# Feed-forward layers: the low parts of the first tile pairs' weights move from VectorE to GpSimd

## What is computed

```python
h = modulate(rms_norm(x, g_ffn1[l]), sh1, sc1)
x = x + 0.5 * ga1[:, None, :] * swiglu(h, w_gate1[l], w_up1[l], w_down1[l])
# swiglu(h, w_gate, w_up, w_down) = (silu(h @ w_gate) * (h @ w_up)) @ w_down
```

## Time and profile before

| | us |
|---|---|
| median of three runs | 2234.31 |
| the profiled execution | 2234.3 |
| its span, first to last instruction | 2232.6 |
| TensorE busy in the span | 2202.2 |
| VectorE busy | 1559.5 |
| ScalarE busy | 1071.6 |
| GpSimd busy | 903.2 |

### The profile page before, as it was taken

The page is one execution under the profiler, slowest core; times in us unless marked ns, Lnnn a source line. Parts: engine busy times, 40 slices in busy tenths (PEclk is TensorE's granted clock), DMA queues, the critical chain, the costliest instruction groups (busy, mean ns, idle before and its releaser), DMA issues.

```text
span 2232.6 us, 29463 instructions
## 1 busy us (share of the span) xinstructions
PE 2202.2 (99%) x10472; PEld 1814.6 (81%) x10472; DVE 1559.5 (70%) x2116; ACT 1071.6 (48%) x2028; POOL 903.2 (40%) x782
## 2 busy tenths in 40 slices
PE   7999999999999999999999999999999999999998
PEld 6888888888887888888787887888778888888887
DVE  7976767578878757732899998578785454547765
ACT  5533333333454553344899898425443333333344
POOL 0044555400122655544557656447205555530013
PEclk9999999999999999999999999999999999999999
DMA  7156565374561533444814065323223222347454
GB/s 281 73 194 221 210 216 202 137 295 165 188 224 50 162 125 137 152 166 141 226 53 119 15 161 152 120 95 142 104 87 126 89 106 103 109 162 262 148 177 160
DMA packets 152033, 338.01 MB, mean 151 GB/s; under 512 B 14224, under 2 KB 36880, under 8 KB 151888
## 3 DMA queue, kind: packets, MB, share of 16 engines
q1 hardware_dynamic: 150624, 333.57, 44.3%
q10 hardware_dynamic: 1264, 2.56, 0.5%
HBM read 247.28 MB, written 86.64 MB: 150 GB/s over the span
## 4 chain that ended last, share of the span: by engine, by line
PE 82%; DVE 11%; ACT 3%; issue 2%; DMA 1%; POOL 1%; SPq 0%; DVEq 0%; ACTq 0%; POOLq 0%
PE ps L3184 11%; PE ps L3185 11%; PE ps L3186 11%; PE ps L3332 6%; PE ps L3330 6%; PE ps L3331 6%; PE ps L3411 4%; PE ps L3413 4%; PE ps L3412 4%; PE ps L3538 3%; PE ps L3563 2%; PE ps L3564 2%; PE ps L3523 2%; PE ps L3142 2%; PE ps L3144 2%
## 5 line engine op out<-in xcount | busy, mean ns | idle before, releaser
L3184 PE MATMUL ps<-r_main,r_z 128*128 128x512 f32 x1232 | 482.0, 391 | 6.1 <-DVE r_main L2212 3.4
L1964 POOL TENSOR_TENSOR r_z<-f_main,r_z 128x512 fp32r<-128x512 f32 x213 | 304.6, 1432 | 446.6 <-ACT r_z L1231 446.6
L3185 PE MATMUL ps<-r_main,r_z 128*128 128x512 f32 x1232 | 480.3, 390 | 0.0
L3186 PE MATMUL ps<-r_main,r_z 128*128 128x512 f32 x1232 | 480.3, 390 | 0.0
L1231 ACT CAST r_z<-f_main 128x512 fp32r<-128x512 f32 x254 | 155.8, 621 | 346.7 <-PE ps L3186 277.5
L3184 PEld LDWEIGHTS ps<-r_main,r_z 128*128 128x128 f32 x1232 | 231.9, 188 | 60.2 <-DVE r_main L2212 4.4
L3186 PEld LDWEIGHTS ps<-r_main,r_z 128*128 128x128 f32 x1232 | 231.8, 188 | 48.2
L3185 PEld LDWEIGHTS ps<-r_main,r_z 128*128 128x128 f32 x1232 | 231.8, 188 | 47.6 <-issue 0.2
L3330 PE MATMUL ps<-r_main 128*128 128x512 f32 x604 | 235.8, 390 | 0.0
L3332 PE MATMUL ps<-r_main 128*128 128x512 f32 x604 | 235.0, 389 | 0.0
L3331 PE MATMUL ps<-r_main 128*128 128x512 f32 x604 | 235.0, 389 | 0.0
(11 more groups left out here) (385 smaller groups left out, 4497.7 us busy)
## 6 DMA issues: line engine op xcount, KB each, us to landing
act_d<-f_main SPq DMA_DIRECT2D x154, 256.0 KB, 2.0
f_main<-act_d SPq DMA_DIRECT2D x70, 512.0 KB, 4.9
f_main<-in_ada SPq DMA_DIRECT2D x56, 512.0 KB, 5.2
f_main<-in_wg SPq DMA_DIRECT2D x20, 1024.0 KB, 5.0
f_main<-in_wu SPq DMA_DIRECT2D x20, 1024.0 KB, 5.0
f_w<-in_wo SPq DMA_DIRECT2D x40, 512.0 KB, 4.0
f_main<-in_wmix SPq DMA_DIRECT2D x18, 1024.0 KB, 5.4
f_e<-in_we SPq DMA_DIRECT2D x10, 1024.0 KB, 5.6
```

The lines of the kernel that those rows point to most:

```text
L1964: pool.tensor_tensor(prod_lo_t[slot], source_of(g), prod_hi_t[slot].bitcast(F32), ALU.subtract).then_inc(s["wl"], 1)
L3184: pe.matmul(out, wh, hi, start=start, stop=False, skip_group_check=True)
L3185: pe.matmul(out, wh, lo, start=False, stop=False, skip_group_check=True)
L3186: return pe.matmul(out, wl, hi, start=False, stop=stop, skip_group_check=True)
```

## The change

VectorE's `first_pair`, used by both layers, loses its 20 `weight_low` calls (`g` = 8 to 27). GpSimd's program starts its loop at 8 in the first layer, and at 0 without a break in the second. The values computed are the same. VectorE still makes `g` = 0 to 7 of the first layer. In `first_pair` one `taken` (UP, product 2) also comes before a `weight_sum`.

```diff
-            pool.wait_ge(fsem[0]["wl"], fbase[0]["wl"] + SECOND + 6)
-            for g in range(SECOND + 6, N_PROD):
+            pool.wait_ge(fsem[0]["wl"], fbase[0]["wl"] + PRELUDE)
+            for g in range(PRELUDE, N_PROD):
                 weight_low(0, g)
...
-            for g in range(PRELUDE):
-                weight_low(1, g)
-            pool.wait_ge(fsem[1]["wl"], fbase[1]["wl"] + SECOND + 6)
-            for g in range(SECOND + 6, N_PROD):
+            for g in range(N_PROD):
                 weight_low(1, g)
...
                     if m >= 12:
                         t1_t3(k, m - 12)
-                        if k == 0:
-                            weight_low(f, m - 4)
...
-                for g in range(8, 12) if k == 2 else ():
-                    weight_low(f, g)
                 for i in range(4):
                     x_low(k, 7, i)
-                weight_low(f, 12)
                 weight_sum(f, 1, UP, 3)
...
                 weight_sum(f, 1, UP, 1)
-                weight_low(f, 13)
-                weight_low(f, 14)
                 for i in range(4):
                     x_low(k, 6, i)
                 weight_sum(f, 1, UP, 2)
-                weight_low(f, 15)
-                weight_low(f, 16)
                 x_low(k, 5, 0)
...
-                weight_low(f, 17)
                 taken(f, AT[1, UP, 6])
                 weight_sum(f, 1, GATE, 4)
-                weight_low(f, 18)
                 weight_sum(f, 1, UP, 4)
-                weight_low(f, 19)
                 taken(f, AT[1, GATE, 5])
-                weight_low(f, 20)
-                weight_low(f, 21)
                 taken(f, AT[1, UP, 5])
...
                     act_sum(f, 0, i)
-                weight_low(f, 22)
+                taken(f, AT[1, UP, 2])
                 weight_sum(f, 2, GATE, 2)
-                weight_low(f, 23)
-                taken(f, AT[1, UP, 2])
                 last_quarter(f, 1)
-                for g in (24, 25, 26):
-                    weight_low(f, g)
                 taken(f, AT[1, UP, 4])
                 weight_sum(f, 2, GATE, 4)
-                weight_low(f, 27)
                 taken(f, AT[1, UP, 3])
```

## The result

The changed kernel takes **2244.0 us**, against 2234.31 before: a ratio of 1.0044, 95% interval 1.0028 to 1.006, that is 6.3 to 13.4 us. The prediction said 2244.3. Four of its runs lie between 2243.63 and 2244.22; a fifth took 4104.97 us at a lower granted clock (0.82) and is left out. The profiled execution took 2244.0 as well. Lines of the code have moved: `piece` is now at L3162 to L3164, `t1_t3` at L2221 and L2222, `t2` at L2229, `t4` at L2235, `x_low` at L2209 and L2212, `weight_sum` 3, 1, 2 and 4 at L2245, L2247, L2251 and L2255, `act_sum` at L2269, `taken` at L2295, L2297 and L2303, `plain_taken` at L2360. GpSimd's `weight_low` is still L1964.

A forecast was written before the change was run, and what follows sets the result against it. TensorE was taken as the bound, its few gaps set by VectorE's full list. Adding +5.2 (first layer), +4.1 (second) and +0.8 (restarts), 10.1 us, to 2234.3 gave 2244.3 us, range 2236 to 2249.5.

The forecast's parts named there:

- What bounds: TensorE, busy 99% of the span, waits in eight gaps for VectorE's full list; at most 4.6 us to gain.
- what an added call does to VectorE: A GpSimd subtraction holds up VectorE steps with two SBUF operands, 1.08 us each; steps reading PSUM keep their length.
- The price of 1.08: Microseconds that one VectorE step with two SBUF operands loses when it meets a GpSimd call.
- The first layer's walk: Engine lists followed forward through the first layer's first pair: TensorE lags 1.3, 1.6, 3.9, 4.9 us, in sum +5.2 us.
- restarts: Each TensorE gap costs 0.08 us more before the next start; some ten gaps more, +0.8 us in all.
- The loads: Pair 2's gate weights load later, moving the cast of 22 from 108.00 to 111.8 us; this costs nothing.
- The second layer: First pair of the second layer: low parts 8 to 11 meet an idle VectorE; loss of +4.1 us.
- The 2.0 us that ScalarE's silu steps were to bring: Second layer, products 22 and 23: silu steps behind the late `act_sum` bring 2.0 us, while gaps of 1.1 fall away.
- The number of collisions: VectorE steps held up by GpSimd calls: 14 counted in the first layer, 10 in the second.
- The full hold: Rival, 12%: each VectorE step held up loses GpSimd's whole 1.25 us; 13.5 us in sum, 2247.8 us.
- Half the collisions: Rival, 10%: only plain subtractions held up, or calls mostly meet PSUM steps and idle time; 2237.5 us.
- VectorE relieved: Rival, 9%: the 12.2 us a layer freed on VectorE's list make up for hold-ups; 2230.9 us.

The follow-up runs named there:

- experiments of 1 and 2: 1: kernel before plus useless GpSimd work, reading SBUF 2261.57 us, only writing 2234.27 us; 2: changed kernel, GpSimd writing zeros for low parts 8 to 27, 2230.32 us.
- experiment 2: The changed kernel, but GpSimd's low parts 8 to 27 are two memsets each in place of the subtraction; 2230.32 us, ratio 0.9983.
- the reading version: The kernel before, VectorE making all low parts, plus a useless GpSimd subtraction reading SBUF for each high part 8 to 27; 2261.57 us, ratio 1.0126.

## Why the prediction was right

**What bounds, and what an added call does to VectorE: right, and shown.** The steps beside GpSimd's calls mostly last 1.67 to 1.78 us in place of 0.69 to 0.74, both plain subtractions and scalar_tensor_tensors; steps with an operand in PSUM keep their length, as the 0.69 at 104.62 beside GpSimd's calls of 102.83 to 108.82. The price of 1.08 was 1.04 to 1.1 in the rows at 71.04 and 72.74. The experiments of 1 and 2 take the cause and the move apart: reads without the move cost 28 us, some 8 of them by the clock; the move without reads gains 3.5.

**The first layer's walk, step by step.** `weight_sum` (UP 2) was to start at 92.6 (2.6 after 90.03) and started at 92.92. Product 15 was to start at 95.5 and started at 95.72; the piece in product 20 at 114.5, it came at 114.62; product 24 at 126.8, it came at 127.22; `weight_sum` (GATE 4) at 124.8, and its row reads 124.09 with 1.76 us, so its undisturbed part (0.69) began at 125.2. The predicted lags of 1.6 and 3.9 and the sum of 5.2 are +1.86 at product 18, +4.05 at 21 and +5.57 at 28 in the table above, restarts included. The layer's sum was 5.2 and half of the 0.8 for restarts, 5.6; measured 5.57, or 5.77 where the execution had no lead. The loads were hidden: the cast of 22, which waits for pair 2's weights, was expected at 111.8 and came at 112.05, and its product did not wait.

**The second layer.** Expected 4.1 and 0.4, measured +4.28. Lows 8 to 11 meet no work of VectorE's, as the 5.05 us at 1618.24 show, and product 24's gap is the one at 1681.24. The 2.0 us that ScalarE's silu steps were to bring at products 22 and 23 are the waits of 0.60 and 1.26 at 1672.95 and 1677.17.

**What was luck, and which terms were off.** That 2244.3 met 2244.0 to 0.3 us is luck in part: the interval of the loss is 6.3 to 13.4 us. The sum was 10.1 us; the time shows 9.7, the two layers' losses in TensorE's starts make 10.1, and no run can tell these apart. The restarts, 0.8 of the sum, were measured by no run alone. The stretched steps cost 14.1 and 10.0 us of VectorE's list where 15.1 and 10.8 were counted, because some met only a part of a call (0.92 us at 112.97, 0.48 at 126.38). The number of collisions was right in sum, not in each place: in the first layer the 128x4 step at 68.07 was one of the 14, and low 12's call stretched no step. The walk let GpSimd have its turn after the step that VectorE was in, and low 12 waited for two (2.30 us). That call ended 0.6 us later than one that waits once, VectorE's `x_low` kept their pace, and `weight_sum` (UP 3) paid with its wait of 1.25 at 83.17.

**The rivals.** The full hold (2247.8) falls by the rows: the longest addition to a VectorE step is 1.12 us, most are 1.04 to 1.1. Its total lies only just above the interval (2240.6 to 2247.7). Where the two engines alternate, VectorE's steps start 1.70 us apart (71.04, 72.74, 74.44), while its 0.61 and GpSimd's whole 1.25 one after the other would be 1.86. The Trainium skill, SBUF — State Buffer, section "Who interferes with whom", has the two engines share a port pair under an exclusive lock, the loser fully blocked. The runs agree with it about which operations meet, and that a GpSimd instruction which only writes doesn't disturb a VectorE one with two SBUF inputs (2234.27 against 2233.84), but the measured price is 1.09 of GpSimd's 1.25 to 1.29. Half the collisions falls: 14 and 10 were there, as counted. VectorE relieved falls because the collisions are there; experiment 2 is that rival made real, 2230.32 where it gave 2230.9.

## What to carry to other kernels

Before moving an elementwise step from VectorE to GpSimd, look in the trace for any pair of rows where the two already overlap, and compare a step's duration there with its duration elsewhere; here a moved call saves 0.61 us of VectorE's list and costs 1.08 in it. By the rows a moved call costs VectorE nothing where VectorE waits, reads PSUM, or GpSimd only writes. Where the list of the busiest helper sets the gaps, look at the order in it too: one call put behind another gained 1.1 us a layer in TensorE's starts (too little for the time to confirm), where moving 40 lost 9.7.

## What the runs showed of the hardware

- **GpSimd doesn't always get the next turn.** Beside back-to-back subtractions of VectorE one of its calls took 2.30 us (1.29 alone) and in the reading version 3.25 (1.04 alone); beside others it took its turn after one step (1.74). What decides is open: other calls beside `x_low` steps did get their turn (the steps of 2.53 and 2.37 us for two at 95.40 and 98.45).
- **A tiny step pays the same.** The 128x4 subtraction at 68.07 took 1.27 us where it met a GpSimd call; elsewhere it takes 0.15.
- **A memset beside it costs VectorE nothing:** 0.53 us each, and four `t2` steps kept 2.73 us.
- **The clock at the start differs between executions:** the granted clock over 20 to 40 us was 1.00 in two of the twelve profiled executions and 0.84 to 0.88 in ten. At product 8 TensorE stood between 1.5 us ahead of the kernel before and 1.3 behind it, though the kernels hardly differ up to there. It is why differences between traces are read here as what TensorE gains or loses within a layer, not as its place at the end.
